# Attention scores of the first block's layers from split q and k, stacked on 128 rows by copies within SBUF

## The reference

```
proj = rmsnorm(x) @ w_in                      # 2048 -> 4608
y_a = conformer_conv(proj[:1024])             # 31 taps over tokens, layer norm, silu
y_b = dilated_attention(q, k, v)              # 16 heads of 64; 3 windows of keys merged
y_c = pool_mixer(proj[4096:])
x = x + rmsnorm(concat(y_a, y_b, y_c) @ w_out)
x = x + rmsnorm((silu(h @ w_gate) * (h @ w_up)) @ w_down)
```

## Time and profile before

| | |
|---|---|
| median of 3 runs | 3277.83 us (3277.53 to 3279.18) |
| the profiled execution | 3278.15 us |
| its span in the trace | 3276.4 us |
| TensorE busy | 3255.2 us, 99% |
| VectorE busy | 2041.8 us, 62% |
| ScalarE busy | 1634.3 us, 50% |
| DMA | 626.70 MB, mean 191 GB/s |
| granted TensorE clock, mean | 0.999 |

### The profile page before, as it was taken

The page is one execution under the profiler, slowest core; times in us unless marked ns, Lnnn a source line. Parts: engine busy times, 40 slices in busy tenths (PEclk is TensorE's granted clock), DMA queues, the critical chain, the costliest instruction groups (busy, mean ns, idle before and its releaser), DMA issues. The chain is left out here.

```text
span 3276.4 us, 43551 instructions
## 1 busy us (share of the span) xinstructions
PE 3255.2 (99%) x16179; PEld 2760.4 (84%) x16179; DVE 2041.8 (62%) x2449; ACT 1634.3 (50%) x2039; POOL 265.0 (8%) x180
## 2 busy tenths in 40 slices
PE   9999999999999999999999999999999999999999
PEld 8888888888888988888888888899898888888887
DVE  6876655555444787665555544477665777777544
ACT  5565544444443556554444444365544655555443
POOL 0000011111000000001111100000000122222000
PEclk9999999999999999999999999999999999999999
DMA  7645677777766664567777776645356677777664
GB/s 230 181 136 166 181 205 206 206 206 202 218 194 193 186 181 129 173 182 204 205 205 206 208 213 197 193 148 174 114 157 205 193 217 211 220 218 217 216 194 162
DMA packets 364799, 626.70 MB, mean 191 GB/s; under 512 B 117912, under 2 KB 120445, under 8 KB 364669
## 3 DMA queue, kind: packets, MB, share of 16 engines
q1 hardware_dynamic: 359693, 615.49, 63.8%
q10 hardware_dynamic: 4976, 9.44, 0.9%
HBM read 599.66 MB, written 2.10 MB: 184 GB/s over the span
## 5 line engine op out<-in xcount | busy, mean ns | idle before, releaser
L1480 DVE TENSOR_TENSOR WL<-WS,WH 128x1024 fp32r<-128x1024 f32 x1120 | 1427.6, 1279 | 1085.9 <-ACT WH L859 1085.1
L859 ACT ACTIVATE WH<-WS 128x1024 fp32r<-128x1024 f32 x1120 | 1186.2, 1061 | 1503.7 <-PE PS L2051 1472.2
L2051 PE MATMUL PS<-WH,XT 128*128 128x512 f32 x5952 | 1829.7, 391 | 0.5 <-ACT XT L874 0.5
L2051 PEld LDWEIGHTS PS<-WH,XT 128*128 128x128 f32 x5952 | 1116.8, 188 | 231.6 <-issue 1.1
L2051 PE MATMUL PS<-WL,XT 128*128 128x512 f32 x2976 | 1128.7, 389 | 0.0
L2051 PEld LDWEIGHTS PS<-WL,XT 128*128 128x128 f32 x2976 | 559.0, 188 | 114.5
L2051 PE MATMUL PS<-WH,HT 128*128 128x512 f32 x2112 | 567.8, 389 | 0.0
L2051 PEld LDWEIGHTS PS<-WH,HT 128*128 128x128 f32 x2112 | 396.3, 188 | 82.3 <-DVE WL L1480 0.2
L2051 PE MATMUL PS<-XT,WH 128*128 128x256 f32 x1792 | 337.0, 287 | 1.6 <-ACT XT L874 1.4
L2051 PE MATMUL PS<-WL,HT 128*128 128x512 f32 x1056 | 327.5, 389 | 0.0
L2051 PEld LDWEIGHTS PS<-XT,WH 128*128 128x128 f32 x1792 | 284.3, 193 | 3.5 <-ACT PR L907 1.5
(11 more groups left out here) (275 smaller groups left out, 1183.8 us busy)
## 6 DMA issues: line engine op xcount, KB each, us to landing
WS<-in_w_in_dram SPq DMA_DIRECT2D x232, 512.0 KB, 3.7
WS<-in_w_gate_dram SPq DMA_DIRECT2D x176, 512.0 KB, 4.4
WS<-in_w_up_dram SPq DMA_DIRECT2D x176, 512.0 KB, 3.9
WS<-in_w_down_dram SPq DMA_DIRECT2D x176, 512.0 KB, 4.5
WS<-in_ffn_up_dram SPq DMA_DIRECT2D x176, 512.0 KB, 4.4
WS<-in_w_out_dram SPq DMA_DIRECT2D x96, 512.0 KB, 4.1
WS<-in_ffn_down_dram SPq DMA_DIRECT2D x88, 512.0 KB, 4.3
T<-in_g_post_mix_dram ACTq DMA_DIRECT2D x4, 512.0 KB, 5.9
```

Source lines behind the costliest of these rows:

```text
L859: act.activation(WH[:, i % RING, :], WS[:, i % RING, :], ACT.Copy).then_inc(s_hi, 1)
L1480: dve.tensor_tensor(WL[:, i % RING, :], WS[:, i % RING, :], WH[:, i % RING, :].bitcast(F32), ALU.subtract).then_inc(s_lo, 1)
L2051: return pe.matmul(o, w, r, start=start, stop=stop, skip_group_check=True)
```

## The change

Each of q and k is split, after the turn, into a high part in fp32r (ScalarE, from PSUM into `qk_hi`) and the remainder, rounded to fp32r (VectorE, PSUM minus high, into `qk_lo`). DMA copies within SBUF then put, for each head, high part and remainder of the same 64 channels on the 128 rows: `q_st` has high above low for one head of a pair and low above high for the other, `k_st` likewise, and `k_sw` has the two parts of k swapped. The product of q_st with k_st gives high by high plus low by low, the product with k_sw the two mixed terms. A head is four fp32r products in place of two fp32 ones. A stack of q is four copies of 64 rows x 4 KB, that of k eight; SP issues them after the loads of unit 36, 41, 64 and 66 (`STACK_AT`). The zeros go, the areas of buffers change, and with them some waits: the rotation of the first k goes from u = 33 to 32, its turn from 35 to 33, the last turn from 59 to 58; T1 and T2 hold parts of q, so the post-norm weights are loaded after unit 66; the zero margins of `upad` are written at u = 67.

```diff
@@ -101,7 +101,8 @@
 TURN_AT = [40 + 2 * h for h in range(8)] + [63 + h for h in range(8)]
 OUTPUT_AT = [41 + 2 * h for h in range(8)] + [65, 66, 67, 68, 69, 70, 71, 71]
 SQUARES_AT = [48, 61, 69, 72]
-ROPE_AT, TURN_QK_AT = (25, 33, 49, 57), [28, 35, 56, 59]
+ROPE_AT, TURN_QK_AT = (25, 32, 49, 57), [28, 33, 56, 58]
+STACK_AT = [36, 41, 64, 66]
 CONV_FROM, MEAN_AT, VAR_AT, RMS_AT, CONV_HIGH_AT, CONV_LOW_AT = 16, 55, 57, 61, 67, 68
 conv_until = lambda u: 0 if u < CONV_FROM else min(11 * (u - CONV_FROM + 1) // 4 if u < 38 else 60 + 4 * (u - 37), 4 * TAPS)
 YB_TURN_AT = YB_LOW_AT = 74
@@ -182,8 +183,12 @@
         pooled = scr(7480, 4, S)
         ycT = scr(8504, 4, S)
         q_nat, k_nat, v_nat = scr(9528, NT, 1024), scr(11576, NT, 1024), scr(13624, NT, 1024)
-        qT = scr(15672, 8, S)
-        k_apart = (scr(17720, 4, 2 * S), scr(6392, 4, 2 * S))
+        rounded = HT[:, :, :, :].rearrange("p a b c -> p (a b c)")
+        stack = lambda at: rounded[:, at:at + 2048].rearrange("p (b n) -> p b n", b=2)
+        q_st, k_st, k_sw = stack(15672), stack(17720), stack(6392)
+        tile_of = lambda v, b, j: v[:, b, j * S:(j + 1) * S]
+        qk_hi = (T1[:, 0:1024].bitcast(F32R), rounded[:, 8504:9528])
+        qk_lo = (T2[:, :].bitcast(F32R), rounded[:, 4216:5240])
         KC = scr(19768, K_END)
         rope = scr(21304, 4, 128)
         pw = scr(21816, 4, P)
...
@@ -355,11 +360,25 @@
                 if turn:
                     turn_planes(sp, turn[1])
 
-            def chunk512(q, w, c, first=False, turn=None):
+            def stack_qk(l, i):
+
+                hi, lo = qk_hi[i % 2], qk_lo[i % 2]
+                sp.wait_ge(s_qkl, 4 * l + i + 1)
+                if i == 2:
+                    sp.wait_ge(s_S, 16 * l + 8)
+                a, b = slice(0, 64), slice(64, 128)
+                for own, swapped, dst in ((hi, lo, (q_st, k_st)[i % 2]), (lo, hi, k_sw))[:1 + i % 2]:
+                    sp.dma_start(dst[a, 0, :].bitcast(F32), own[a, :].bitcast(F32)).then_inc(s_qkd, 16)
+                    sp.dma_start(dst[b, 0, :].bitcast(F32), swapped[a, :].bitcast(F32)).then_inc(s_qkd, 16)
+                    sp.dma_start(dst[a, 1, :].bitcast(F32), swapped[b, :].bitcast(F32)).then_inc(s_qkd, 16)
+                    sp.dma_start(dst[b, 1, :].bitcast(F32), own[b, :].bitcast(F32)).then_inc(s_qkd, 16)
+
+            def chunk512(q, w, c, first=False, turn=None, after=lambda i: None):
 
                 for i in range(8):
                     load(q, i, w[2 * i * P:(2 * i + 2) * P, c].rearrange("(k p) n -> p k n", p=P), CHUNK,
                          turn if turn and i == turn[2] else None)
+                    after(i)
                     if first and i == 0:
                         sp.wait_ge(s_eps, 1)
                         layer_rows(0)
@@ -439,7 +458,8 @@
                 for n, c in enumerate(IN_ORDER):
                     if (l, n) == (0, 1):
                         sp.dma_start(C[:, 2 * P:C_END], a["constants"][:, 2 * P:C_END]).then_inc(s_const2, 16)
-                    chunk512(q + 2 * n, w, slice(c * CHUNK, (c + 1) * CHUNK), l + n == 0)
+                    chunk512(q + 2 * n, w, slice(c * CHUNK, (c + 1) * CHUNK), l + n == 0,
+                             after=lambda i: [stack_qk(l, k) for k in range(4) if STACK_AT[k] == 8 * n + i])
                 q1 = q + U_IN1 // 4
                 out_proj(q1, a["w_out"][l])
                 q2 = q1 + U_OUT // 4
@@ -535,19 +555,14 @@
                 act.wait_ge(s_lna, 3 * l + 1)
                 act.wait_ge(s_ssb, 8 * l + 2)
                 act.activation(sq, acc, ACT.Square).then_inc(s_sqr, 1)
-            if u in TURN_QK_AT[:3]:
+            if u in TURN_QK_AT:
                 i = TURN_QK_AT.index(u)
-                half = i // 2
                 act.wait_ge(s_qkt, 4 * l + i + 1)
-                if i % 2 == 0:
-                    act.activation(flat(qT[:, 4 * half:4 * half + 4, :]), flat(PS[:, TURN_QK_BANK[i]:TURN_QK_BANK[i] + 2, :]),
-                                   ACT.Copy).then_inc(s_qk, 1)
-                else:
-                    act.wait_ge(s_pad, l + 1)
-                    for b in range(2):
-                        rows = slice(64 * b, 64 * b + 64)
-                        ins = act.activation(k_apart[half][rows, :, b * S:(b + 1) * S], quad(TURN_QK_BANK[i])[rows, :, :], ACT.Copy)
-                    ins.then_inc(s_qk, 1)
+                if i == 0:
+                    act.wait_ge(s_glu, l + 1)
+                if i >= 2:
+                    act.wait_ge(s_qkd, 384 * l + 192)
+                act.activation(qk_hi[i % 2], flat(PS[:, TURN_QK_BANK[i]:TURN_QK_BANK[i] + 2, :]), ACT.Copy).then_inc(s_qk, 1)
             if u == VAR_AT:
                 root_of_sums(1, SUM_BANK)
                 next_table(ACT.Silu)
@@ -977,6 +992,9 @@
                             copy_scale(2 * l)
                         if i < 7:
                             mixers_act(act, l, 8 * c + i)
+                        if (c, i) == (8, 2):
+                            act.wait_ge(s_qkd, 384 * (l + 1))
+                            load_post_weight(a["g_post_mix"][l:l + 1])
                     if c == 1:
                         act.wait_ge(s_freeT, ti + 2)
                         act.activation(f3(T1), gT, ACT.Sigmoid).then_inc(s_sg, 1)
@@ -990,10 +1008,6 @@
                             ins = act.activation(dst[:, t, half * 512:(half + 1) * 512], PS[:, base + t, :], ACT.Copy,
                                                  scale=(rinv8 if n % 3 == 0 else rinv)[:, t:t + 1])
                         ins.then_inc(s_freeN, 1)
-                    if c == 3:
-
-                        act.wait_ge(s_glu, l + 1)
-                        load_post_weight(a["g_post_mix"][l:l + 1])
                     mixers_act(act, l, 8 * c + 7)
                 for u in range(U_IN1, U_IN1 + KT):
                     split(q, u + RING)
@@ -1074,12 +1088,15 @@
             if u == MEAN_AT - 1:
                 dve.wait_ge(s_cv, CONV_STEPS * l + 4 * TAPS)
                 sum_of_tiles(dve, acc, s_cv, CONV_STEPS * l + 4 * TAPS + 1)
-            if u == TURN_QK_AT[3]:
-                dve.wait_ge(s_qkt, 4 * l + 4)
-                for b in range(2):
-                    rows = slice(64 * b, 64 * b + 64)
-                    ins = dve.tensor_copy(k_apart[1][rows, :, b * S:(b + 1) * S], quad(TURN_QK_BANK[3])[rows, :, :])
-                ins.then_inc(s_qk, 1)
+            if u - 1 in TURN_QK_AT:
+                i = TURN_QK_AT.index(u - 1)
+                dve.wait_ge(s_qk, 4 * l + i + 1)
+                dve.tensor_tensor(qk_lo[i % 2], flat(PS[:, TURN_QK_BANK[i]:TURN_QK_BANK[i] + 2, :]), qk_hi[i % 2].bitcast(F32),
+                                  ALU.subtract).then_inc(s_qkl, 1)
+            if u == 67:
+                dve.wait_ge(s_qkd, 384 * (l + 1))
+                dve.memset(upad[:, :, 0:8], 0.0)
+                dve.memset(upad[:, :, 8 + S:UP], 0.0).then_inc(s_pad, 1)
             for k, at in enumerate((VAR_AT - 1, RMS_AT - 2, POOL_RMS_AT - 1)):
                 if u == at:
                     dve.wait_ge(s_sqr, 9 * l + 3 * k + 1)
@@ -1646,12 +1663,8 @@
                 norm_in(2 * l, G_PRE, q, after)
                 ti = l * T_LAYER
 
-                for v in (hpad[:, :, 0:15], hpad[:, :, 15 + S:HP], upad[:, :, 0:8], upad[:, :, 8 + S:UP]):
+                for v in (hpad[:, :, 0:15], hpad[:, :, 15 + S:HP]):
                     dve.memset(v, 0.0)
-                for k_of in k_apart:
-                    dve.memset(k_of[64:128, :, 0:S], 0.0)
-                    ins = dve.memset(k_of[0:64, :, S:2 * S], 0.0)
-                ins.then_inc(s_pad, 1)
                 for c in range(9):
                     for i in range(8):
                         u = 8 * c + i
@@ -1800,7 +1813,7 @@
                     pe.wait_ge(s_pt, 16 * l + 8)
                     pe.wait_ge(s_yb, 4 * l + 2)
                 if i == 3:
-                    pe.wait_ge(s_qk, 4 * l + 3)
+                    pe.wait_ge(s_qkl, 4 * l + 3)
                 for j in range(4):
                     for t in range(NT):
                         b = TURN_QK_BANK[i] + j // 2
@@ -1821,14 +1834,16 @@
                 last.then_inc(s_o, 1)
             for h in heads_at(SCORES_AT, u):
                 if h % 8 == 0:
-                    pe.wait_ge(s_qk, 4 * l + h // 4 + 2)
+                    pe.wait_ge(s_qkd, 384 * l + 192 * (h // 8 + 1))
                 if h == 9:
                     pe.wait_ge(s_std, 3 * l + 2)
                 if h:
                     pe.wait_ge(s_sb, 16 * l + (h if h < 8 else h - 1))
-                k_of = k_apart[h // 8][:, h // 2 % 4, (h % 2) * S:(h % 2 + 1) * S]
-                for t in range(NT):
-                    last = mm(PS[:, score_bank(h), t * S:(t + 1) * S], qT[:, h // 2, t * P:(t + 1) * P], k_of, True, True)
+                q, k, k_other = (tile_of(v, h % 2, h // 2 % 4) for v in (q_st, k_st, k_sw))
+                for t in range(NT):
```

(5 more changed lines are left out.)

## The result

The changed kernel takes 3293.51 us (median of 5 runs, 3290.63 to 3295.81) against 3277.83 before: a ratio of 1.0046, 95% interval 1.0034 to 1.0058. That is 15.7 us more. The forecast of 3285.2 had the sign and the order of the causes, but the time lies 2.5 us above the upper end of its range.

What follows compares the result with a forecast made beforehand. TensorE's program order was taken as the bound. From 3278.15 us, 12.2 saved on scores, less 1.8 at head 9, 6.9 for turns and 10.6 for copies, gave 3285.2; range 3272 to 3291.

Steps and rivals of the forecast that it cites:

- What bounds the kernel: Whole kernel: TensorE, busy 3255.2 of 3276.4 us, sets the time; its savings come off and each new wait adds.
- Scores: Each head's score products on TensorE: 0.48 us in place of 0.86, 0.38 saved, 12.2 us over 32 heads.
- the optional 0.08 a head: Scores: the first product after fp32 work comes some 0.08 us late, which on every head would leave 9.6 saved.
- Head 9: Before head 9's transposes: TensorE waits for ScalarE's exponential, losing 0.9 us a layer, 1.8 in all.
- Turns: Turns of k after units 33 and 58: TensorE waits 2.0 and 1.45 us for VectorE's rotation, 6.9 in all.
- Price of a copy: Stack copies of 256 KB over 64 rows: 1.15 us each, between ends of 0.64 and 1.28, plus 2.4 fixed.
- Issues: SP's issuing of k's copies: 0.37 us for an issue, so 8 are out in 3.0 us.
- the second half's wait: Before scores of head 8: copies need 11.6 us against 7.05 of cover, so TensorE waits 4.55 a layer.
- rival 2: Copies at full half rate behind a weight load, or TensorE's clock dropping after a 5 us wait: 3291.8 us, chance 0.12.
- the clock: TensorE's granted clock after a long wait: taken to stay at 1.00, nothing in the sum; a drop stood in rival 2.
- the signs of an error: Prediction wrong if copies land within 8 us, TensorE doesn't wait at the turns, or its clock leaves 1.00 after a wait.
- Rivals 1, 3, 4: 1: copies at loads' rate, 3275.6 (0.27); 3: heads stay 0.86 us, 3295.7 (0.04); 4: cheap turns, fast copies, 3269.5 (0.07).

Runs made afterwards that it cites:

- run 4: Changed kernel with the first k's rotation at the start of VectorE's step 32 and the second's in step 55, not 57; 3293.44 us, ratio 1.0052 to the kernel before.
- run 2: Changed kernel with the same bytes in half as many copies, each over 128 rows, no halves swapped; 3278.99 us, ratio 1.0005 to the kernel before.
- run 1: Changed kernel with each stack copy cut to 32 of its 1024 columns, the rest of the stacks zero; 3276.20 us, ratio 0.9998 to the kernel before.
- run 6: Changed kernel with rotation and turns of k back where the kernel before has them, k's copies behind them; 3316.94 us, ratio 1.0121 to the kernel before.
- run 9: Run 8's kernel with k's low part ahead of the weight split, in the turn's own step; 3285.08 us, ratio 1.0023 to the kernel before.
- run 11: Run 8's kernel with both k's low part ahead of the weight split and k's copies one load earlier; 3276.01 us, ratio 0.9995 to the kernel before.
- run 7: Changed kernel with parts written straight to their own stack rows, 6 copies a half in place of 12; 3278.92 us, ratio 1.0005 to the kernel before.
- run 8: Changed kernel with the halved copies of run 7 and the earlier k rotations of run 4; 3273.98 us, ratio 0.9989 to the kernel before.
- run 10: Run 8's kernel with k's copies one weight load earlier in SyncE's order; 3280.03 us, ratio 1.0007 to the kernel before.

## Why the prediction was off

**What bounds the kernel**: right, TensorE's order. "Each new wait of TensorE is added, wherever it stands" holds for the sum, but not for taking one away: where a later wait has its own source, it grows by as much (run 4).

**Scores**: right. 0.48 us a head, 0.38 saved, 12.2 in all; the optional 0.08 a head did not appear. **Head 9**: a wait of 0.66 before the transposes in place of 0.9, 1.3 us for both layers against 1.8.

**Turns**: right. 1.88 and 1.24 us against 2.0 and 1.45, released by the rotation; 6.3 against 6.9. They come from VectorE's order, as worked out: with the rotations ahead they fall to 0.5 to 0.7.

**Price of a copy**: right within a tenth. 262 KB at 236 to 250 GB/s is 1.05 to 1.11 us; I had taken 1.15. That a copy would be slow because SBUF is read and written was not so (run 2); the covered rows alone are the cause. The Trainium skill's rule ("SBUF — State Buffer", section "Door 1: The DMA port swizzle") that partitions 0 to 63, or 64 to 127, reach half of the ports gave an estimate of 1.2. The traces agree with its direction (236 to 250 GB/s against 404 to 412, run 2), with 58 to 61% of the rate and not half.

**Issues**: "8 are out in 3.0" was wrong. The eight took 7.7 us to issue (207.36 to 215.09), 7.4 in the first half. No run shows a cost of its own for this: from 208 us on the DMA engines had a share of 0.98 or more, and small copies, issued 0.6 us apart, brought no wait (run 1).

**The step that failed is the second half's wait**, "8 copies need 2.4 + 9.2 = 11.6 us: TensorE waits 0.75 in the first half and 4.55 in the second". It took the queue as empty at the first issue and the copies as evenly spaced. In the first half that held: the eight landed after 11.3 us, and the cover was 11.1 to 11.3 (scores 0 start at 128.88), so TensorE waits for some 0.2 us. In the second it did not. The eight copies landed after 13.7 us (13.3 in the second layer) and not 11.6. Cover was 7.3 us (7.05 predicted), the wait 6.43 (6.02). By the prediction's terms the first copy lands at 2.4 + 1.15 = 3.55 us; it landed at 4.6, 1.0 later. The seven others should need 8.05 us and took 9.1, and the last alone took 2.6 of them. For the first delay the trace shows what stood ahead: q's four copies, 4.3 us by the same price, and two loads, issued from 199.70 on; the second of the loads, issued before the copies, landed only at 213.03. Why the last copy came late no run settles; in run 6, where q's copies lay further back, it did not. The weight load ahead stood in rival 2; q's copies, which I had priced in bytes for themselves, stood in no queue of mine. That the copies' waits came out near as a sum, 12.4 against 10.6, is in part luck: the 1.5 us forecast for the first halves hardly came, and 3.35 too little stood in the second ones.

**The other miss is the clock**, 4.3 us, which the sum put at nothing. It was in rival 2 and among the signs of an error, with 0.12 for both. Rival 2 gave 3291.8 with 17.1 us for copies (its own terms make the second wait 6.87 and not 6.75, so 3292.0), and the stated range ended below it, at 3291. The profiled execution has 12.4 + 4.3 = 16.7, at 3291.86, by other parts: no wait in the first half, where the rival had 1.8. That the two times agree is luck. Without the clock the profiled execution would stand near 3287.6, inside the range. So the mechanism was right, and the terms that were mis-sized are the second wait (by 1.9 and 1.5 in the two layers) and its echo in the clock (0 taken, 2.34 and 1.96 measured).

**Rivals 1, 3, 4**: the copies do not run as fast as loads (run 2 shows the condition under which they would: 128 rows), a head did not stay at 0.86, the turns were not cheap.

## What to carry to other kernels

A copy within SBUF is priced by the rows it covers and by what stands ahead of it in the queue when it is issued, not by its bytes alone: count the copies and loads issued shortly before (here within 8 us), then the cover. Write a result to its final rows from the engine that makes it and copy only what must cross to other rows (the copies' 16.7 us with the clock became 1.4 here, though the turns' wait grew from 6.3 to 9.0); a wait gained at one place can be worth nothing until the next wait of the same chain is gone too. Before moving one engine's work forward, look at what the moved-past step gives back, since a queue that is issued in order turns a late buffer into a late copy (run 9), and a copy put ahead of a load into a late load (run 11).

## What the runs showed of the hardware

- With full DMA engines, copies over 64 rows moved 236 to 250 GB/s, over 128 rows 404 to 412 (run 2), both ends in SBUF.
- Eight copies of 256 KB over 64 rows land 11.3 us after the first issue with little ahead of them, and 13.7 with q's four copies and two loads issued in the 7.7 us before.
- An instruction over 64 rows takes as long as over 128: VectorE's subtraction is two of 64x1024 in 2.46 us (run 9) against 1.22 for one of 128x1024 (run 4).
- SyncE's issue of a copy takes 0.47 us for the first of a stack and up to 1.94 us for a later one (201.71 above).
- TensorE's granted clock fell to 0.50 in the waits of 6.43 and 6.02 us and stayed there for 4 to 5 us of full work behind them, which cost 2.34 and 1.96 us. After shorter waits it did either. It stayed at 1.00 after 2.60 us (run 7, second turn), after 1.69 us (run 2, scores 8) and after 1.88 us (the first turn of the changed kernel). It fell after that same wait of 1.88 us in run 2, after 1.87 and 1.90 us in run 8, and after 1.82 us in the second layer of run 10 but not in the first. So the length of such a wait doesn't decide it, and what does these runs don't settle. The executions of run 8 took 3272.0 to 3277.5 us, with mean clocks of 1.000 and 0.998 at the two ends.
